# Eleven RMS norms: squares summed on TensorE, context beside x, input in four pieces, two result tiles side by side

## What is computed

```python
def rms_norm_2(x, g):
    xf = x.astype(jnp.float32)
    y = xf * lax.rsqrt(jnp.mean(xf * xf, axis=-1, keepdims=True) + EPS)
    return (y * g.astype(jnp.float32)).astype(x.dtype)
...
        hl = modulate(rms_norm_2(x, norm1_g[i]), ml[0], ml[1])
        ...
            hc = modulate(rms_norm_2(h_ctx, norm1_g[i]), mc[0], mc[1])
        # mixer: attention, neighbourhood attention, convolution or Fourier, by i
        x = x + ml[2] * yl
        x = x + ml[5] * sq_relu_mlp(modulate(rms_norm_2(x, norm2_g[i]), ml[3], ml[4]), mlp_w1[i], mlp_w2[i])
    return rms_norm_2(x, final_g)
```

## Time and profile before

| | us |
|---|---|
| median of 3 runs | 4478.17 (4477.41 to 4478.62) |
| the profiled execution | 4478.1 |
| its span | 4476.3 |
| TensorE busy | 4145.3 (93%) |
| DVE busy | 1810.6 (40%) |
| ScalarE busy | 952.3 (21%) |
| GpSimd busy | 423.4 (9%) |
| mean granted TensorE clock | 0.947 |

### The profile page before, as it was taken

The page is one execution under the profiler, slowest core; times in us unless marked ns, Lnnn a source line. Parts: engine busy times, 40 slices in busy tenths (PEclk is TensorE's granted clock), DMA queues, the critical chain, the costliest instruction groups (busy, mean ns, idle before and its releaser), DMA issues. The chain is left out here.

```text
span 4476.3 us, 40622 instructions
## 1 busy us (share of the span) xinstructions
PE 4145.3 (93%) x15976; PEld 2609.6 (58%) x15976; DVE 1810.6 (40%) x3020; ACT 952.3 (21%) x2062; POOL 423.4 (9%) x264
## 2 busy tenths in 40 slices
PE   8998979799998899999989888999999999899998
PEld 3354445244554455565545455888544788747886
DVE  3553337443276022111010493665173566304433
ACT  1140016232155021100010352201132202112020
POOL 0000000011000000000000001111130111101112
PEclk8999969689999899999999999999999999999999
DMA  3103320202100222322111211444110344212221
GB/s 129 63 20 112 134 69 2 85 1 71 37 25 9 46 76 94 113 83 106 57 57 38 73 36 38 169 169 141 66 57 19 132 157 163 80 57 71 80 94 38
DMA packets 207675, 343.04 MB, mean 77 GB/s; under 512 B 19904, under 2 KB 77664, under 8 KB 207456
## 3 DMA queue, kind: packets, MB, share of 16 engines
q1 hardware_dynamic: 188176, 320.42, 20.6%
q10 hardware_dynamic: 17136, 10.07, 0.9%
q0 software_dynamic: 2176, 9.96, 0.8%
HBM read 334.41 MB, written 6.03 MB: 76 GB/s over the span
## 5 line engine op out<-in xcount | busy, mean ns | idle before, releaser
L1154 PE MATMUL psum<-H,ring 128*128 128x512 f32 (+1 forms) x2608 | 1149.9, 601 | 32.8 <-issue 16.3
L1154 PEld LDWEIGHTS psum<-H,ring 128*128 128x128 f32 (+1 forms) x2608 | 496.7, 192 | 667.9 <-issue 654.9
L1282 PE MATMUL psum<-arena,ring 128*128 128x256 f32 x1536 | 343.3, 380 | 2.8 <-ACT arena L1562 2.8
L1908 DVE SCALAR_TENSOR_TENSOR arena<-ring,cond,arena 128x512 f32<-128x512 f32 x448 | 320.0, 752 | 8.0
L1282 PEld LDWEIGHTS psum<-arena,ring 128*128 128x128 f32 x1536 | 290.4, 190 | 44.0 <-ACT arena L1562 5.2
L1282 PE MATMUL psum<-arena 128*128 128x256 f32 x1152 | 255.5, 379 | 0.0
L2097 DVE TENSOR_REDUCE small<-psum 128x1 f32<-128x768 f32 (+7 forms) x352 | 203.8, 613 | 112.4 <-PE psum L1341 49.7
L2287 POOL TENSOR_TENSOR ring<-ring 128x1024 f32<-128x1024 f32 x48 | 162.4, 3383 | 815.4 <-DVE arena L1798 815.4
L1653 ACT ACTIVATE arena<-psum,small 128x768 f32<-128x768 f32 (+7 forms) x336 | 204.3, 613 | 160.3 <-DVE small L2097 126.0
L1891 DVE TENSOR_TENSOR mods<-psum,vec 128x4 f32<-128x4 f32 (+1 forms) x48 | 7.7, 161 | 569.2 <-PE psum L1122 568.3
L1282 PEld LDWEIGHTS psum<-arena 128*128 128x128 f32 x1152 | 218.9, 190 | 29.8
(11 more groups left out here) (210 smaller groups left out, 4721.2 us busy)
## 6 DMA issues: line engine op xcount, KB each, us to landing
ring<-in_mlp_w SPq DMA_DIRECT2D x64, 2048.0 KB, 7.9
ring<-in_ada_w SPq DMA_DIRECT2D x48, 2048.0 KB, 7.9
ring<-in_na_qkv SPq DMA_DIRECT2D x6, 2048.0 KB, 7.8
ring<-in_pw SPq DMA_DIRECT2D x6, 2048.0 KB, 7.9
ring<-in_ab_in SPq DMA_DIRECT2D x5, 2048.0 KB, 7.9
ring<-in_cd_in SPq DMA_DIRECT2D x4, 2048.0 KB, 7.7
ring<-in_at_qkv SPq DMA_DIRECT2D x3, 2048.0 KB, 8.5
ring<-in_ab_out SPq DMA_DIRECT2D x2, 2048.0 KB, 7.8
```

Of the source, the lines that this page charges most:

```text
L1154: last = nc.tensor.matmul(out, lhs, rhs, start=(k == 0), stop=(k == len(t.pairs) - 1))
L1282: last = nc.tensor.matmul(out, w[:, i, P * m:P * m + P], x[:, i, :], start=(opens and m == 0 and i == 0), stop=(i == k - 1), skip_group_ch ...
L1908: ins = nc.vector.scalar_tensor_tensor(partial[:, v, :], w[:, k, :], cond[:, k, v:v + 1], partial[:, v, :], ALU.mult, ALU.add)
```

## The change

- **Sums.** In every norm of x all eight tiles of squares are summed by TensorE, each with four one-column matmuls (32 matmuls in the place of 4). GpSimd adds nothing.
- **Context beside x.** The context's norm is part of the stage of x's norm: its sum goes first, into bank 7; its root, reciprocal, scaling and shifts follow those of x. ScalarE squares the tiles of both in the order in which they are done. In the projection after the first attention the second group makes the context's tiles first.
- **Keep-busy matmuls.** After the sums TensorE runs four matmuls of 256 columns on a constant, and after the spreading one five more (`keep_busy`, `BUSY`).
- **Input in four pieces.** X comes in four DMAs with a semaphore each. Vectors and identity go to ScalarE's queue, as do the first stage's two tables, which now belong to stage 0; masks, sinks and context follow three weight blocks on SP's. ScalarE's and DVE's small preparations come after the first norm. The first norm is like the others.
- **Two tiles side by side.** A projection behind a norm makes its first two tiles together, k by k, and the chased products of a fast stage go over k outside and their two halves inside.
- **Sums of weights ahead.** DVE makes the first fast unit's `weight_sums` in the stage before the norm, after its seventh residual tile.
- ScalarE and GpSimd no longer meet the others before a norm.

```diff
+BUSY = (4, 5)
...
-        def norm(src, dst, n, gain, shift=None, sq=None):
-
-            stage("norm", src=src, dst=dst, n=n, gain=gain, shift=shift, sq=sq)
+        def norm(gain, shift=None, sq=None, ctx=None, loads=()):
+            stage("norm", gain=gain, shift=shift, sq=sq, ctx=ctx, loads=list(loads))
...
-            norm(X, H, S, sg(1, 0), mod(layer, 3, 0), sq=low_arena)
-            norm(CX, CH, C, sg(1, 1), mod(layer, 3, 1))
+            norm(sg(1, 0), mod(layer, 3, 0), sq=low_arena,
+                 ctx=(sg(1, 1), mod(layer, 3, 1), arena[:, 12288:12288 + KD * C].rearrange("p (t s) -> p t s", s=C)))
...
         def at_out(b, c0, c1):
-            out = []
-            out += residual_tiles(b, c0, c1, X, H, S, mod(0, 2, 0))
-            out += residual_tiles(b, c0, c1, CX, CH, C, mod(0, 2, 1))
-            return out
+            own = residual_tiles(b, c0, c1, X, H, S, mod(0, 2, 0))
+            of_ctx = residual_tiles(b, c0, c1, CX, CH, C, mod(0, 2, 1))
...
+                stages[s_ - 2]["sums_for"] = st["units"][0]
...
+            for i, arrived in enumerate(x_in):
+                sp.dma_start(X[:, 2 * i:2 * i + 2, :],
+                             dram["x"][2 * i:2 * i + 2].rearrange("k p s -> p k s")).then_inc(arrived, 16)
                 if b == RING:
+                    for dst, src in ((arena[:, 0:P], dram["diag_mask"]), (arena[:, P:2 * P], dram["prev_mask"]),
+                                     *((sinks[HD * half:HD * half + HD, g, :], dram["sinks"][HD * g:HD * g + HD])
+                                       for half in range(2) for g in range(2))):
+                        sp.dma_start(dst, src).then_inc(inputs_in, 16)
                     sp.dma_start(CX[:, :, :], dram["ctx"].rearrange("k p s -> p k s")).then_inc(context_in, 16)
...
+                    paired = st["chases"] and waited == 0 and all(len(t.pairs) == KD and t.out[2] == S for t in tiles[:2])
+                    for made in ([tiles[:2]] if paired else []) + [[t] for t in tiles[2 * paired:]]:
+                        for t in made:
+                            open_bank(t.bank)
+                        for k in range(len(made[0].pairs)):
+                            for t in made:
+                                lhs, rhs = t.pairs[k]
+                                last = nc.tensor.matmul(psum[part:part + rows, t.bank * BANK:t.bank * BANK + cols], lhs,
+                                                        rhs, start=(k == 0), stop=(k == len(t.pairs) - 1))
+                                if k == len(t.pairs) - 1:
+                                    last.then_inc(tile_ready, 1)
...
+            def keep_busy(count):
+
+
+                b = min(range(PROJ_BANKS), key=lambda x: opened.get(x, -1))
+                if b in bank_freed:
+                    pe.wait_ge(*bank_freed[b])
+                for _ in range(count):
+                    nc.tensor.matmul(bank(b, 2 * P), mean_d[:, :], mean_d[:, :].unsqueeze(1).to_broadcast([P, 2, P]),
+                                     start=True, stop=True)
...
-                        for m in range(u["mt"]):
-                            out = bank(at, HALF, HALF * m)
-                            for i in range(k):
-                                if u["chase"] and m == 0 and p < 3:
+                        chased = u["chase"] and p < 3
+                        for m, i in [(m, i) for i in range(k) for m in range(u["mt"])] if chased else \
+                                [(m, i) for m in range(u["mt"]) for i in range(k)]:
+                            if chased and m == 0:
+                                pe.wait_ge(norm_ready, st["norm_x"] + (p - 1) * k + i + 1)
...
-                if st["sq"] is not None:
-                    pe.wait_ge(sumsq_ready, n["sumsq"] + 1)
-
-                    for i in range(ST):
-                        last = nc.tensor.matmul(bank(6)[:, i:i + 1], st["sq"][:, 0, P * i:P * i + P], mean_d[:, 0:1],
-                                                start=(i == 0), stop=(i == ST - 1), skip_group_check=True)
-
-                    pe.wait_ge(rstd_diagonal, n["sumsq"])
-                    nc.tensor.matmul(bank(6), mean_d[:, :], rstd[:, :], start=True, stop=True).then_inc(rstd_ready, 1)
+                if st["ctx"] is not None:
+                    open_bank(7)
+                    for k in range(KD):
+                        pe.wait_ge(ctx_squares, st["ctx0"] + k + 1)
+                        last = nc.tensor.matmul(bank(7, C), mean_d[:, :], st["ctx"][2][:, k, :], start=(k == 0),
+                                                stop=(k == KD - 1))
+                    last.then_inc(ctx_mean, 1)
+                    bank_freed[7] = (ctx_sd, st["ctx0"] // KD + 1)
+                open_bank(6)
                 for k in range(KD):
+                    for i in range(ST):
+                        last = nc.tensor.matmul(bank(6)[:, i:i + 1], st["sq"][:, k, P * i:P * i + P], mean_d[:, 0:1],
+                                                start=(k == 0 and i == 0), stop=(k == KD - 1),
+                                                skip_group_check=True)
+                n["sumsq"] += 1
+                keep_busy(BUSY[0])
+                pe.wait_ge(rstd_diagonal, n["sumsq"])
+                nc.tensor.matmul(bank(6), mean_d[:, :], rstd[:, :], start=True, stop=True).then_inc(rstd_ready, 1)
+                bank_freed[6] = (norm_ready, st["norm0"] + KD)
+                if st["index"] + 1 < len(stages):
+                    keep_busy(BUSY[1])
...
+                squares = [(st["x_done"].get(k, 0), 1, k) for k in range(KD)]
+                if st["ctx"] is not None:
+                    squares += [(st["cx_done"].get(k, 0), 0, k) for k in range(KD)]
                     act.wait_ge(context_in, 16)
+                for done, of_x, k in sorted(squares):
+                    if st["index"] == 0:
+                        act.wait_ge(x_in[k // 2], 16)
+                    if done:
+                        act.wait_ge(dve_took, done)
+                    if of_x:
+                        nc.scalar.activation(st["sq"][:, k, :], X[:, k, :], ACT.Square).then_inc(squares_ready, 1)
+                    else:
+                        nc.scalar.activation(st["ctx"][2][:, k, :], CX[:, k, :], ACT.Square).then_inc(ctx_squares, 1)
+                if st["ctx"] is not None:
+                    n["ctx"] += 1
+                    act.wait_ge(ctx_mean, n["ctx"])
+                    nc.scalar.activation(sd[:, C:2 * C], bank(7, C), ACT.Sqrt, bias=eps).then_inc(ctx_sd, 1)
...
+                    if st["ctx"] is not None:
+                        for k in range(KD):
+                            act.wait_ge(scaled_ready, n["scaled"] + k + 1)
+                            nc.scalar.activation(CH[:, k, :], CH[:, k, :], ACT.Identity,
+                                                 bias=st["ctx"][1](k)).then_inc(norm_ready, 1)
...
+                if st["index"] == 0:
+                    act.wait_ge(inputs_in, 16 * N_INPUTS)
+                    act.wait_ge(vec_in, 16)
+                    act.wait_ge(ident_in, 16)
...
+            act.dma_start(vec[:, :], dram["vectors"]).then_inc(vec_in, 16)
+            act.dma_start(ident[:, :], dram["ident"]).then_inc(ident_in, 16)
+            act.wait_ge(constants_made, 5)
...
+                        if t.tile == KD - 2 and "sums_for" in st:
+                            weight_sums(st["sums_for"])
...
+                    if st["ctx"] is not None:
+                        dve.wait_ge(ctx_sd, st["ctx0"] // KD + 1)
+                        chain(nc.vector.reciprocal(sd[:, C:2 * C], sd[:, C:2 * C]))
+                        for k in range(KD):
+                            nc.vector.scalar_tensor_tensor(CH[:, k, :], CX[:, k, :], st["ctx"][0](k), sd[:, C:2 * C],
+                                                           ALU.mult, ALU.mult).then_inc(scaled_ready, 1)
...
-                follows = st["kind"] in ("prep", "conv") or (st["kind"] == "norm" and st["sq"] is not None)
-                if s == 0 or not follows:
+                if st["kind"] not in ("prep", "conv", "norm"):
                     gate(pool, "pool", s)
-                if st["kind"] == "norm" and st["sq"] is not None:
-
-                    N = st["n"]
-                    for k in range(1, KD):
-                        pool.wait_ge(squares_ready, st["sq0"] + k + 1)
-                        if k > 1:
-                            pool.wait_ge(pool_steps, pool_count)
-                        ins = nc.gpsimd.tensor_tensor(st["sq"][:, 0, 0:N], st["sq"][:, 0, 0:N], st["sq"][:, k, 0:N],
-                                                      ALU.add)
-                        if k < KD - 1:
-                            ins.then_inc(pool_steps, 1)
-                            pool_count += 1
-                        else:
-                            ins.then_inc(sumsq_ready, 1)
```

(59 more changed lines are left out.)

157 lines of the change are left out of this document (65 added, 92 removed).

## The result

The changed kernel takes 4502.2 us (median; 4489.0 to 4504.6 in 5 runs), the kernel before 4477.4 beside it: ratio 1.0049, 95% interval 1.0037 to 1.0062. Timed once more beside experiments on another occasion it took 4492.3 (4489.1 to 4494.8, 5 runs) against 4475.7: 1.0036 (1.0024 to 1.0049). It is slower, by 17 to 25 us; I had said 4487, 9 us slower. The profiled execution is the longest of the five, 4504.6 (span 4501.4).

What follows compares the result with a forecast made beforehand. TensorE, busy for 93% of the span, bounds the kernel, so only its idle or half-clock time can be won. Terms by norm plus the pairing sum to +8.9 us on 4478.1, giving 4487; own range 4476 to 4502.

Steps and rivals of the forecast that it cites:

- the third product: Fast stages behind norms 5, 7, 9: ScalarE instead of DVE holds this product; +3.6, +2.7, +2.7 us.
- The length of the sums: TensorE's 64 one-column matmuls per norm: 9.4 us, the clock falling 4.0 us after the last wide matmul.
- earliest fall: Case of the clock falling 2.1 us after the last wide matmul: nine norms lose 1.9 us each, total 4504.
- Norm 1: Norm behind a modulation: DVE held until 398.1, so the 10.0 us sums hide behind it; -0.5 us.
- What follows the sums: Keep-busy matmuls and spread, 4.9 us, plus 2.3 for the clock's return, up to the next stage's first tile.
- Norm 0: Start of the kernel: x in four pieces, first landing at 5 us, first tile at 26.4; -7.0 us (-9 to -5).
- the pairing: Two tiles side by side in the first and gqa stages: wait for copy and square, +1.5 us each, +3.0 together.
- Never falls: Rival for TensorE's sums: the clock stays full under them, 6.7 us each; -38 us, total 4440; chance 0.13.
- Weight loads that don't slow down: Rival for the narrow sums: weight loads keep their time in a fallen clock; total 4454; chance 0.04.
- The keep-busy matmuls don't bring it back: Rival behind the sums: next stage starts at half clock, +4.8 us in ten norms, about 4532; chance 0.06.
- GpSimd's relief hides nothing else: Around the norms: GpSimd was idle there, so taking its adds away gains nothing further; no us given.

Runs made afterwards that it cites:

- e6: Changed kernel in which the first square waits for all four pieces of x; 4503.0 us, ratio 1.0061.
- e3: Changed kernel without two result tiles side by side, the first two tiles behind a norm made one after the other; 4492.4 us, ratio 1.0033.
- e2: Changed kernel with one keep-busy matmul of 256 columns between the sums of each two tiles of squares; 4537.5 us, ratio 1.0135.
- e1: Changed kernel with GpSimd adding the squares of tiles 1 to 7 onto tile 0 again, TensorE summing only that one; 4445.4 us, ratio 0.9925.
- e8: Changed kernel with each tile of squares summed in one wide matmul, no diagonal or spread, more keep-busy matmuls; 4447.6 us, ratio 0.9933.
- e7: From e1: squares shared between GpSimd and TensorE, no two tiles side by side, keep-busy counts changed in norms 0 and 1; 4416.7 us, ratio 0.9869.
- e9: e7 with three keep-busy matmuls before the spread instead of four, one or two before the last tile in norms 5, 7, 9; 4411.9 us, ratio 0.986.

## Why the prediction was right and where it was off

The mechanism was right in its main parts: the clock falls under the narrow sums, the keep-busy matmuls and the spread bring it back before the next stage, DVE no longer holds the third product, and the start is earlier. It came out slower, as forecast. The sum was 16 us too small in the profiled execution (+25.1 in the span against +8.9) and 8 in the repetition. Of the 16, norms 1 to 10 make 10.9, norm 0 makes 1.5, and the stretches between the norms 3.8. Term by term in the first:

- **The length of the sums is the term that was mis-sized.** I took 9.4 us (10.0 in norm 1), from a fall 4.0 us behind the last wide matmul. Measured, norms 1 to 10: 13.2, 11.4, 9.9, 9.0, 11.3, 10.8, 11.3, 10.8, 11.6, 10.7. The ten excesses make 15 us. Since a sum takes 13.5 us less the time at full clock, 10.99 means 2.5 us at full clock, not 4.0; over the six profiles that have these sums the mean is 10.5, or 3.0. The 4.0 was a mean over norms of the kernel before in which TensorE stood idle, and it ranged there from 2.1 to 5.4; I took its middle as if it were a constant. Its early end, 2.1, was in the earlier trace rows, and my own working gave 4504 for it: the first profile is close to that "earliest fall", which I had counted as a margin, and the repetition, at 4492, lies between it and my forecast. Why the fall comes 1 us earlier under narrow work than in idle time is open (the idle side is one profile of ten norms), and so is the moment in a given execution.
- **Norm 1.** I put its fall at 5.3 us, as before. It fell at 384.6, 2.2 us behind the last wide matmul and 0.7 into the sums, and the 16 ones-matmuls (1.84 us) that come between did not put it off: 13.2 in the place of 10.0. In the other five profiles it fell there after 2.4 us four times and once after 4.5. DVE's modulation sums ended at 394.3, so the sums, which I had hidden behind DVE, set the end: +2.4 against my -0.5.
- **What follows the sums** was right: 6.1 to 7.7 us from their end to the first tile where I said 7.2, 15.6 to 16.0 to the third product where I said 15.8. The clock came back 2.7 to 6.0 us behind the end of the sums, 4.2 in the mean, where I said 4.6. Norm 6 came to -0.3 (said -0.4), norm 10 to +1.6 (+1.5), norm 3 to +3.7 (+3.8); norms 8, 5, 7, 9, 2 to +0.4, +5.5, +4.6, +4.6, +4.3 (-1.4, +3.6, +2.7, +2.7, +2.2), mostly by the length of their sums; norm 4 to -3.0 (-1.3).
- **Norm 0**: the first square at 5.66 (said 5), the sums end at 20.2 (19.2), the first tile at 27.9 (26.4), -5.5 in the place of -7.0. Pieces 3 and 4 landed together at 12.2; the first two pieces bought 7 us, as e6 shows.
- **The stretches between the norms** lost 6.8 us, where I had 3.0 for the pairing. Of it 2.4 lie between norms 0 and 1 and 3.5 between 2 and 3, where head norms ride. But the pairing's wait is 0.7 us in the first and nothing in the second, as the timelines above show, so this term was wrong: behind norm 2 a DMA ends the wait, and I had left it out. The other 6 us are not explained. Between the two profiles of the changed kernel and that of e3 the three stretches between norms 0 and 3 differ by 3.8, 3.4 and 1.5 us, the middle one, to which I gave nothing, as much as the others.
- **The rivals.** "Never falls" is out: the clock fell in each of ten norms. "Weight loads that don't slow down" is out: the same instruction took 1.71 and 0.95 us for eight (e2). "The keep-busy matmuls don't bring it back" is out, by the 1.00 in three windows behind the start of the next stage (its own sum was off: +4.8 in ten norms makes 4535, not 4532). "GpSimd's relief hides nothing else" was right and is the point: e1 gives GpSimd its adds back and wins 47 to 57 us.

The costliest thought was missing altogether: I compared the new sums with the wait that they replace and never asked for another shape. By my own numbers eight wide matmuls would have cost 6.9 us, and e8 shows that the clock holds under them.

## What to carry to other kernels

Work moved onto TensorE behind a stage is paid for in the clock as well as in its own time: ask which shape it has. One-column matmuls keep the engine busy in the profile and let the clock fall to half; wide ones of the same length hold it (e8, 7.0 to 7.1 us every time). All adds on an idle GpSimd (e1, 4445) and all sums in wide matmuls (e8, 4448) came out alike here, and sharing was best (e7 and e9, 4417 and 4412): TensorE got only what GpSimd could not finish in time. 16 one-column instructions with a few wide ones around them passed without a fall in norms 5, 7 and 9 of e9, but in e7 only in norm 7 of these. And where a cost depends on the moment of a switch of the clock, give it the range that the trace shows, its early end included, and not its mean.

## What the hardware showed that I had not expected

- Wide matmuls of 0.5 us between narrow runs of 0.8 us didn't hold the clock; it fell 4.9 us behind the last stage in norm 5 in the place of 2.4, and 3.5 to 8.8 in norms 5 to 10 (e2). The page "TensorE: Matmul & The Clock Gate" of the Trainium skill says in "HAM oscillation — how this bites in real kernels" that idle gaps are what makes the clock fall. Here TensorE had no gap, in the changed kernel (busy for 8.00 of 8.00 us behind the last wide matmul) and in e2 (14.60 of 14.60), and it fell.
- The same 64 instructions at the same place took 8.7 us in one execution of the changed kernel and 11.3 in the other (norm 7). The kernel before ranged over 3 us in its first five runs (8 over all occasions), the changed one over 16. That ten such places make up this difference is likely, but not shown.
